# The feed-forward of a transformer kernel in two phases: all up products first, then the down product by output tile

## The reference, cut to what matters

```python
D_MODEL, SEQ, D_FF = 1024, 256, 2816
def rms_norm(x, g):
    return x * lax.rsqrt(jnp.mean(x * x, axis=-1, keepdims=True) + EPS) * g
def swiglu(h, w_gate, w_up, w_down):
    return (jax.nn.silu(h @ w_gate) * (h @ w_up)) @ w_down
...
    x = x + 0.5 * swiglu(rms_norm(x, ffn_norm[l, 0]), ffn_w_gate[l, 0], ffn_w_up[l, 0], ffn_w_down[l, 0])
    h = rms_norm(x, mix_norm[l])
    x = x + mixer(h)
    x = x + 0.5 * swiglu(rms_norm(x, ffn_norm[l, 1]), ffn_w_gate[l, 1], ffn_w_up[l, 1], ffn_w_down[l, 1])
```

## Time and profile before

| what | value |
|---|---|
| timed executions, median of 3 | 2423.82 us |
| profiled execution, its span | 2429.0 us |
| TensorE busy | 2406.8 us |
| VectorE busy | 1780.5 us |
| ScalarE busy | 1130.4 us |
| mean granted clock of TensorE | 0.995 |

### The profile page before, as it was taken

How to read it: one execution, slowest core, us unless ns; L and a number is a source line. 1 busy time by engine, 2 the same in 40 slices (tenths; PEclk the granted TensorE clock), 3 DMA queues, 4 the chain that set the end, 5 groups by cost and what they waited for, 6 DMA issues and landing times.

```text
span 2429.0 us, 39962 instructions
## 1 busy us (share of the span) xinstructions
PE 2406.8 (99%) x16772; PEld 2216.2 (91%) x16772; DVE 1780.5 (73%) x2178; ACT 1130.4 (47%) x1317; POOL 74.7 (3%) x106
## 2 busy tenths in 40 slices
PE   8999999999999999999999999999999999999999
PEld 7999899999999978999999988989999999888998
DVE  8778745877877878778776766587787777666876
ACT  5335544433433664334335764443343367544432
POOL 2000000000000010100000000001000000000000
PEclk9999989999999999999999999999999999999999
DMA  6555335555555425655554533466555555344554
GB/s 214 190 181 169 119 118 177 179 186 190 177 188 190 153 75 177 215 187 179 191 186 146 173 120 124 160 193 207 189 182 183 189 159 169 109 139 156 183 183 137
DMA packets 308139, 409.43 MB, mean 169 GB/s; under 512 B 9798, under 2 KB 274464, under 8 KB 308000
## 3 DMA queue, kind: packets, MB, share of 16 engines
q1 hardware_dynamic: 304736, 401.66, 51.7%
q0 software_dynamic: 3072, 5.69, 0.8%
q10 hardware_dynamic: 192, 0.08, 0.0%
HBM read 406.35 MB, written 1.05 MB: 168 GB/s over the span
## 4 chain that ended last, share of the span: by engine, by line
PE 97%; DVE 1%; ACT 1%; issue 0%; DMA 0%; ACTq 0%; DVEq 0%
PE acc L637 25%; PE bank L575 24%; PE bank L1044 17%; PE bank L578 13%; PE bank L1042 3%; PE acc L2349 2%; PE acc L575 1%; PE bank L601 1%; PE bank L2873 1%; PE bank L594 1%; PE acc L2366 1%; PE acc L2467 1%; PE acc L578 1%; PE bank L2321 1%; PE bank L1234 0%; PE bank L2632 0%
## 5 line engine op out<-in xcount | busy, mean ns | idle before, releaser
L476 ACT ACTIVATE part_hi<-raw 128x2048 fp32r<-128x2048 f32 (+1 forms) x382 | 726.5, 1906 | 916.9 <-DMA raw<-in_ffn_w 383.3
L483 DVE TENSOR_TENSOR part_lo<-raw,part_hi 128x2048 fp32r<-128x2048 f32 (+1 forms) x382 | 868.1, 2277 | 245.8 <-ACT part_hi L476 242.6
L575 PE MATMUL bank<-hT,part_hi 128*128 128x512 f32 x2560 | 641.6, 392 | 0.0
L575 PEld LDWEIGHTS bank<-hT,part_hi 128*128 128x128 f32 x2560 | 460.9, 189 | 83.0
L637 PE MATMUL acc<-gated,part_hi 128*128 128x256 f32 x2816 | 519.9, 283 | 0.0
L637 PEld LDWEIGHTS acc<-gated,part_hi 128*128 128x128 f32 x2816 | 445.1, 192 | 0.0
L1044 PE MATMUL bank<-part_hi,hT 128*128 128x256 f32 (+1 forms) x2336 | 439.6, 287 | 0.2
L637 PE MATMUL acc<-gated,part_lo 128*128 128x256 f32 x1408 | 398.5, 283 | 0.0
L1044 PEld LDWEIGHTS bank<-part_hi,hT 128*128 128x128 f32 x2336 | 372.2, 194 | 6.4 <-issue 4.7
L578 PEld LDWEIGHTS bank<-hT,part_lo 128*128 128x128 f32 x2560 | 349.2, 190 | 24.9
L578 PE MATMUL bank<-hT,part_lo 128*128 128x256 f32 x2560 | 356.9, 282 | 0.0
(11 more groups left out here) (465 smaller groups left out, 2228.1 us busy)
## 6 DMA issues: line engine op xcount, KB each, us to landing
raw<-in_ffn_w SPq DMA_DIRECT2D x132, 1024.0 KB, 5.2
raw<-in_w_in SPq DMA_DIRECT2D x52, 1024.0 KB, 5.3
raw<-in_ffn_w_up SPq DMA_DIRECT2D x44, 1024.0 KB, 5.3
raw<-in_ffn_w_down SPq DMA_DIRECT2D x44, 1024.0 KB, 4.9
raw<-in_ffn_w_gate SPq DMA_DIRECT2D x43, 1024.0 KB, 5.3
raw<-in_hy_w_in SPq DMA_DIRECT2D x22, 1024.0 KB, 5.2
raw<-in_hy_w_out SPq DMA_DIRECT2D x8, 1024.0 KB, 4.9
raw<-in_w_out SPq DMA_DIRECT2D x8, 1024.0 KB, 5.0
```

The lines of the kernel that those rows point to most:

```text
L476: t.e.activation(part_hi[:, n % SLOTS, 0:size], raw[:, n % SLOTS, 0:size], ACT.Copy).then_inc(hi_ready, 1)
L483: t.e.tensor_tensor(part_lo[:, n % SLOTS, 0:size], raw[:, n % SLOTS, 0:size], part_hi[:, n % SLOTS, 0:size].bitcast(F32), ALU.subtract).th ...
L575: pe.matmul(b.rearrange("p (h s) -> p h s", h=2), slot_cols(s, 0)[:, k, f * P:(f + 1) * P], hT[:, :, k, :], start=(k == 0), stop=False, sk ...
```

## The change

The feed-forward is cut the other way. First all 22 up pieces run: gate and up products of chunk after chunk alternate between bank and acc. ScalarE copies the low half of each product out of PSUM, VectorE adds the high half, multiplies by the root row, and the gated values of all chunks are kept in ff (both parts, 22 tiles). Then come 12 down pieces: for each of four pairs of output tiles, three pieces of 8, 8 and 6 tiles of the down weight's rows. ffn_down uses the shape of the up product, one 512-column matmul for the high weight by both parts and one of 256 for the low weight. While TensorE makes the next pair, ffn_down_scalar and ffn_down_vector add a finished pair to xT, make hT and the squares. The last pair is taken tile by tile. Before a mixer and before a following feed-forward these take the place of pre_scalar and pre_vector; after a mixer those stay. A feed-forward now has 34 pieces in place of 33, the last of each pair smaller. ffn_up_first has another order. The final transposes of the first three pairs stand between down pieces. The loops are written out. Two tensors of the first mixer change places, and a memset of xbc moves into that mixer.

```diff
-FFN_PIECES = [SLOT] * (3 * CHUNKS)
+FFN_UP = 2 * CHUNKS
+FFN_PIECES = [SLOT] * FFN_UP + [COLS * (k1 - k0) for _ in range(4) for k0, k1 in DOWN_KS]
...
         def up_banks(c, which):
-            return (acc if (c, which) == (1, 0) else bank)[:, 2 if c == 1 else 2 * which:4 if c == 1 else 2 * which + 2, :]
+            return (acc if c % 2 else bank)[:, 2 * which:2 * which + 2, :]
...
+        def down_banks(b):
+            return (acc, bank, bank, acc)[b][:, (0, 0, 2, 2)[b]:(2, 2, 4, 4)[b], :]
...
+            for f in range(2):
+                narrow(f, range(0, KD - 2))
+                both(f, range(0, KD - 2))
+            for k in (KD - 2, KD - 1):
+                for f in range(2):
+                    narrow(f, (k,))
+                for f in range(2):
+                    mm = both(f, (k,))
             mm.then_inc(piece_done, 1)
...
+        def ffn_down(t, k, b, s, ks, on_first=None):
+            pe = t.e
+            for f in range(2):
+                out = down_banks(b)[:, f, :]
+                for i in ks:
+                    pe.matmul(out.rearrange("p (h s) -> p h s", h=2), slot_cols(s, 0)[:, i - ks.start, f * P:(f + 1) * P],
+                              ff[:, :, i, :], start=(i == 0), stop=False, skip_group_check=True)
+                for i in ks:
+                    mm = pe.matmul(out[:, 0:S], slot_cols(s, 1)[:, i - ks.start, f * P:(f + 1) * P], ff[:, 0, i, :],
+                                   start=False, stop=(i == FF_K - 1), skip_group_check=True)
+                if on_first and f == 0:
+                    on_first(mm)
             mm.then_inc(piece_done, 1)
...
             root_row_tensor(t)
...
+            done = CHUNKS * k
+            for c in range(1, CHUNKS):
                 for which in range(2):
+                    s = arrived(t)
+                    if c == 1 and which == 0:
                         pe.wait_ge(acc_taken, 4 * t.acc_uses)
+                        pe.wait_ge(root_row_ready, t.roots)
+                    if c > 1:
+                        pe.wait_ge(up_out if which else gate_out, done + c - 1)
+                    ffn_up(t, c, s, which)
...
+            for b in range(4):
+                for j, (k0, k1) in enumerate(DOWN_KS):
+                    s = arrived(t)
+                    if j == 0:
+                        pe.wait_ge(*room[b])
+                    if b == 0:
+                        pe.wait_ge(gated_ready, done + (k1 + 1) // 2)
+                    split_end = b == 3 and j == len(DOWN_KS) - 1
+                    ffn_down(t, k, b, s, range(k0, k1), (lambda mm: mm.then_inc(first_full, 1)) if split_end else None)
+                    if k == 7 and b and j == 0:
+                        out_flip_tensor(t, b - 1)
...
         def ffn_scalar(t, k):
+            for c in range(CHUNKS):
+                n = CHUNKS * k + c
+                v = silu_gate[:, c % 2, :]
+                act.wait_ge(piece_done, SLOTS + p + 2 * c + 1)
+                if c:
+                    act.wait_ge(gate_out, n)
+                else:
+                    act.wait_ge(sums_ready, 3 * (k // 2) + 2 * (k % 2) + 1)
+                act.activation(low_rows[:, 0, :, :], low_of(up_banks(c, 0)), ACT.Copy).then_inc(gate_low, 1)
+                next_hi(t)
                 if c == 0:
...
                     root_row_scalar(t)
+                act.wait_ge(gate_scaled, n + 1)
                 act.activation(v, v, ACT.Silu).then_inc(silu_ready, 1)
...
+                act.activation(low_rows[:, 1, :, :], low_of(up_banks(c, 1)), ACT.Copy).then_inc(up_low, 1)
+                next_hi(t)
+                act.wait_ge(gate_made, n + 1)
+                act.activation(ff[:, 0, 2 * c:2 * c + 2, :], v.rearrange("p (f s) -> p f s", f=2), ACT.Copy)\
+                    .then_inc(gated_hi, 1)
...
+        def ffn_down_scalar(t, at):
+            for b in range(4):
+                next_hi(t)
+                next_hi(t)
...
+                else:
+                    act.wait_ge(first_full, t.see(first_full))
+                    low_out(0, 1)
+                    if at is not None:
+                        act.wait_ge(first_ready, t.see(first_ready))
+                        high(2 * b)
+                    act.wait_ge(piece_done, SLOTS + t.piece + 1)
+                    low_out(1, 2)
+                    act.wait_ge(x_ready, t.see(x_ready))
+                    if at is not None:
+                        high(2 * b + 1)
+                if at is not None:
+                    act.activation(square_rows[:, b, :, :], xT[:, 2 * b:2 * b + 2, :], ACT.Square).then_inc(x_squares, 1)
+            next_hi(t)
...
         def ffn_vector(t, k):
+            for c in range(CHUNKS):
+                n = CHUNKS * k + c
+                v = silu_gate[:, c % 2, :].rearrange("p (f s) -> p f s", f=2)
+                dve.wait_ge(piece_done, SLOTS + p + 2 * c + 1)
+                dve.wait_ge(gate_low, n + 1)
+                dve.tensor_tensor(v, high_of(up_banks(c, 0)), low_rows[:, 0, :, :], ALU.add).then_inc(gate_out, 1)
                 if c == 0:
+                    next_lo(t)
                     root_col_vector(t)
                     dve.wait_ge(root_row_ready, t.see(root_row_ready))
...
+                dve.tensor_tensor(v, v, root_rows(2), ALU.mult).then_inc(gate_scaled, 1)
                 if c:
+                    next_lo(t)
...
+                dve.tensor_tensor(v, up_rows, v, ALU.mult).then_inc(gate_made, 1)
+                next_lo(t)
+                dve.wait_ge(gated_hi, n + 1)
+                dve.tensor_tensor(ff[:, 1, 2 * c:2 * c + 2, :], v, ff[:, 0, 2 * c:2 * c + 2, :].bitcast(F32), ALU.subtract)\
...
+        def ffn_down_vector(t, at):
+            def added(k0, k1, sig):
+                v, f0, f1 = xT[:, k0:k1, :], k0 % 2, k0 % 2 + k1 - k0
+                dve.wait_ge(down_low, t.see(down_low))
+                dve.scalar_tensor_tensor(v, high_of(down_banks(b))[:, f0:f1, :], 0.5, v, ALU.mult, ALU.add)\
+                    .then_inc(down_added, 1)
+                dve.wait_ge(down_added, t.see(down_added))
+                dve.scalar_tensor_tensor(v, down_rows[:, f0:f1, :], 0.5, v, ALU.mult, ALU.add).then_inc(sig, 1)
+                dve.wait_ge(sig, t.see(sig))
...
             for n in range(4):
-                if n:
-                    pre_scalar(t, FFNS[2 * n][3])
                 ffn_scalar(t, 2 * n)
-                pre_scalar(t, MIXERS[n][0])
+                ffn_down_scalar(t, MIXERS[n][0])
                 MIXERS[n][3](t, *MIXERS[n][5])
                 pre_scalar(t, FFNS[2 * n + 1][3])
                 ffn_scalar(t, 2 * n + 1)
+                ffn_down_scalar(t, None if n == 3 else FFNS[2 * n + 2][3])
```

More of the change, by code:

```diff
@@ L38 @@
 SLOT = 2048
-LOOP = 12
 COLS = 256
 CHUNKS = FF // COLS
+FF_K = FF // P
+DOWN_KS = ((0, 8), (8, 16), (16, FF_K))
 SSD_W = 1024
@@ L206, in two_blocks @@
         with ExitStack() as m:
-            gated = sb("gated", [P, 2, 2, 512], F32R, where=m)
+            branch = sb("branch", [P, 2, 4, S], F32R, where=m)
         with ExitStack() as m:
@@ L250, in two_blocks @@
         with ExitStack() as m:
+            ff = sb("ff", [P, 2, FF_K, S], F32R, where=m)
+        with ExitStack() as m:
             xbc = sb("xbc", [P, CONV_T, CONV_K - 1 + S], where=m)
@@ L497, in through, with arrived @@
             return SLOTS + t.piece
[L499 to L504, removed]
+        def arrived(t):
+            n = t.piece
+            t.piece += 1
+            t.e.wait_ge(lo_ready, n + 1)
             return n % SLOTS
@@ L586, in ffn_up_first, with narrow, both @@
             pe = t.e
-            for f in range(2):
[L588 to L608, removed]
+            def narrow(f, ks):
+                for k in ks:
+                    if f == 0:
+                        hi_k(k)
+                    pe.matmul(up_banks(0, 0)[:, f, 0:S], slot_cols(s, 1)[:, k, f * P:(f + 1) * P], hT[:, 0, k, :],
+                              start=(k == 0), stop=False, skip_group_check=True)
+            def both(f, ks):
+                for k in ks:
+                    if f == 0:
+                        both_k(k)
+                    mm = pe.matmul(up_banks(0, 0)[:, f, :].rearrange("p (h s) -> p h s", h=2),
+                                   slot_cols(s, 0)[:, k, f * P:(f + 1) * P], hT[:, :, k, :], start=False,
+                                   stop=(k == KD - 1), skip_group_check=True)
+                return mm
+            for f in range(2):
+                narrow(f, range(0, KD - 2))
[5 more added lines that the diff above has]
+                    mm = both(f, (k,))
             mm.then_inc(piece_done, 1)
@@ L661, in ffn_tensor @@
             root_row_tensor(t)
-            n0 = t.piece
-            for j in range(2):
+            done = CHUNKS * k
+            for c in range(1, CHUNKS):
                 for which in range(2):
-                    s = arrived(t, None, n0 + 3 * j + which)
-                    if j + which == 0:
+                    s = arrived(t)
```

(24 more changed lines are left out.)

205 lines of the change are left out of this document (110 added, 95 removed).

## The result

The changed kernel takes 2444.55 us (median of four executions, 2440.89 to 2451.95) where the kernel before took 2423.75 in the same job: ratio 1.0084, 95% interval 1.0073 to 1.0096. It is 20.8 us slower; the prediction said 14.7 slower, 2438.5 us, in a range of 2428 to 2454.

What follows compares the result with a forecast made beforehand. TensorE, busy in 99% of the span, was taken as the bound. Terms of 17.65 us less and 32.2 more gave net 14.6 more on 2423.8: say 2438.5 us, own range 2430 to 2447, widened to 2428 to 2454.

Steps and rivals of the forecast that it cites:

- down product: Down pieces of eight feed-forwards: one wide matmul for two narrow saves 0.010 us, 14.4 us less; bounds nothing and 15.0.
- first pieces: First piece of a feed-forward: shorter waits for hT, 2.25 us less after feed-forwards and 1.0 less after mixers.
- root, after a mixer (4): Feed-forward start after a mixer: TensorE stalls 3.95 us for root column and row, four times, 15.8 us more.
- root, after a feed-forward (3): Start after a feed-forward, T its last matmul's end: VectorE free at T + 8.3, stall 2.95 us, three times, 8.9 more.
- root, first: Start of the first feed-forward: the late root chain and root row cost 2.5 us more.
- mixers' starts (4): Start of a mixer: wait for k = 7's high part grows by 0.8 us, four times, 3.2 more.
- the end: Kernel's end: 12 transposes between down pieces cost 1.3 us, the last half tile 0.5; loss 1.8 us.
- falls of the clock: Rival: TensorE's clock falls in the root pause at seven starts, 2.0 us each, 14 us, giving 2454; chance 0.2.
- Up phase and DMA: Up phase in steady state: VectorE's 8.7 us fits TensorE's 11.2 per pair; weight pieces hidden with 0.3 us in hand; no stall.
- a hidden stall: Rival: VectorE reaches the root chain no later than now, only the root row's round trip stays, 2420 us; chance 0.07.
- no change: Rival: no measurable change, root stalls about half the forecast's, 1.6 to 2.2 us a start; chance 0.06.
- no saving: Rival: the wide down matmul saves nothing, or weights come late, 14.4 us more, 2453; chance 0.07.

Runs made afterwards that it cites:

- the sixth experiment: Kernel with root chain first on VectorE and odd chunks' banks exchanged, plus the down product's 512-column matmul taken apart into two of 256: 2423.33 us.
- the first: Changed kernel with the root chain put back in front of the gate's add and the split on VectorE: 2419.12 us, ratio 0.9983 to the kernel before.
- second: Changed kernel with only the banks of the odd chunks exchanged (gate in acc 2 and 3, up in acc 0 and 1): 2435.88 us, ratio 1.0061.
- fourth experiments: Kernel before the change with one edit: in chunk 0 of ffn_vector the split stands in front of the root chain: 2450.40 us, ratio 1.0100.
- the last experiment: Kernel with root chain first and odd chunks' banks exchanged, plus the last tile pair's second split moved behind the last low part: 2408.84 us, ratio 0.9940.
- dummy work: Changed kernel with dummy 512-column matmuls on TensorE in front of the wait for root_col: 2438.83 us, ratio 1.0051.

## Why the prediction was right, point by point

The sign, the place and the mechanism were right. That the time came out within 6.1 us of the forecast is partly luck, as two errors went against each other. The profiled terms, without the clock's falls, against the forecast:

| term | forecast | measured |
|---|---|---|
| down product | -14.4 | -15.0 (8 x 1.87) |
| first pieces | -3.25 | -2.8 (3 x 0.75, 4 x some 0.13) |
| root, after a mixer (4) | +15.8 | +14.6 (3.65 each, at k = 3) |
| root, after a feed-forward (3) | +8.9 | +7.0 (k = 2: 2.42) |
| root, first | +2.5 | +3.0 |
| mixers' starts (4) | +3.2 | +2.7 (0.71, 0.74, 0.63, 0.57) |
| the end | +1.8 | +0.8 |
| sum | +14.6 | +10.3 |
| falls of the clock | a rival, 14 us, chance 0.2 | +9.7 in the profiled run |

With the falls that is 20.0 us. The 9.5 us that the profiled execution of before lost in its mixers, and 0.4 us less until the end of the kernel's very first piece, lead from there to the 10.1 us between the two spans. So the table leaves next to nothing of the spans open.

**The down product** came out at 15.0, the upper bound, and the sixth experiment shows that it is the width, with the weight load that a merged pair saves, and not the order of the pieces. (That bound was put at a run of 2.79 us, which would give 15.8; 15.0 is a run of 2.795.) **Up phase and DMA**: no wait for a weight piece turned up in either phase; VectorE and ScalarE fitted in.

**The first pieces after a mixer** gave half of what I took: the wait for the low parts of k = 4 and 5 takes the place of nearly the whole of the old one.

**The root** was the step that decided, and the first, second and fourth experiments show both halves of it apart: VectorE's order (16.0 us of listed waits) and the bank (0.8 us a start). After a feed-forward I had VectorE free at T + 8.3; it was at T + 8.0 with T = 620.00, and the stall 2.42 instead of 2.95. The path to that moment is the one forecast: the split that waits for its piece starts at 617.80 and ends at T + 0.09, the high part of k = 7 starts at T + 2.87 and ends at T + 3.4.

**The mixers' starts** behaved as forecast, and the last experiment shows that the deferred split takes the waits away. **The end** cost less than I took, since the transposes of three pairs, 0.36 us each, are taken off the tail.

**The clock** is the term that was mis-sized. I took it as all or nothing, beside the forecast. It comes start by start: in the profiled execution it costs 1.6 (k = 0), 2.8, 2.5 and 2.8 us (k = 1, 5, 7), 2.4 a fall where I had taken 2.0. The forecast of 14.7 lies 6.1 us under the measured 20.8: the falls that it left out are 9.7, and the other terms, 4.3 too high together, hid a part of that. Half of the rival belonged into the likeliest sum; with it, 2438.5 would have been some 2445.5. That 10.3 + 9.7 = 20.0 us is close to the 20.8 of the medians is partly chance, since every timed execution has its own falls, in the mixers too. The mean granted clock goes with the time (0.994 at 2440.89 us, 0.990 at 2451.95, 0.992 at the two between), so the falls make the spread of 11 us; where they lie in the executions that were not profiled is not known. The rivals of a hidden stall, of no change and of no saving did not happen.

**Slips in the working.** The starts' lower bound of 16 us gives 2427 and not 2430. No change would have been stalls of 1.0 to 2.2 us a start, by the limit of 1 us that the rival before it has. The parts add up to 0.87 for slower and 0.07 for faster. None of them moves the forecast or its range.

## What to carry to other kernels

When the bound engine is 99% busy, look at what it will wait for, not at what it will have less of: an order of instructions on an engine with idle time cost more here than 1408 matmuls saved. Before an instruction is put in front of another on a helper engine, follow who waits for the second one and how much slack the trace shows; here it was 0.25 us. And a pause of about 2 us or more on TensorE can cost more than its length, because the clock may fall behind it, here by 1.6 to 2.8 us more.

## What the runs showed of the hardware

The same pause doesn't always have the same effect. In the changed kernel the waits for root_col at k = 1, 3, 5, 7 are alike (2.57 to 2.62 us, then 0.57), and behind k = 3 the clock stayed at 2.4 GHz while it fell behind the others. In the old kernel with the late root a shorter pause, 1.9 us and no second one, was followed by a fall at five starts in a row and at none of the first three. Pauses of 1.1 to 1.4 us (the changed kernel, k = 2, 4, 6) and a single wait of 0.57 us (the root chain first) or 0.56 us behind dummy work were followed by one at no start in the profiles. Falls are not tied to these pauses alone: every profile of the case, that of before too, has some in the mixers, and their number differs from one to the next. What tells the pauses apart is not settled by these runs.
